# The recurrent stage's order of work: the next pair's chunk products and three of its masks ahead of the scan over states, the query products in other PSUM space

## The chip, the cores and the metric

One core of a Trainium2 chip runs the whole program. The metric is device time in microseconds. The kernel before has a median of 4070.77 us over 3 runs (4065.65 to 4073.46).

## The reference, cut to what matters

The reference is two transformer blocks of width 2048 over 256 latent tokens with 256 context tokens. The first block's token mixer has an RWKV-7 branch, which is computed in both directions for 16 heads of 64 channels. For each token the state `S` of a head is decayed, corrected and added to, and then read out:

```python
def step(S, inp):
    r_t, w_t, k_t, v_t, kk_t, a_t = inp
    sa = jnp.einsum('bhvk,bhk->bhv', S, -kk_t)
    S = (S * w_t[:, :, None, :] + sa[..., None] * (kk_t * a_t)[:, :, None, :]
         + v_t[..., None] * k_t[:, :, None, :])
    y = jnp.einsum('bhvk,bhk->bhv', S, r_t) if emit else None
```

Both blocks also need modulation vectors, `silu(c) @ w_ada + b_ada`, whose weight matrices are large (2048 x 12288 and 2048 x 6144 in float32) and are multiplied with two condition vectors only. The other parts (attention, feed-forward, the second block) are not touched by the change.

## The kernel before, in words

The program is one block with a hand-written instruction list per engine. The stage that the change touches is the recurrent one, some 650 us long (about 740 to 1390 us of the span). Its loop has eight passes, `for it in range(8)`; each handles a pair of heads (128 partitions, 64 per head) over 512 tokens (context and latents) and is called a pair here. The two directions are `d` = 0 and 1.

The tokens are cut into 8 chunks of 64 (`CH`), so that the recurrence becomes, per direction:

- `from_keys(d)` (L1107, L1112) and `chunk_pairs(d)` (L1069): products of scaled keys within a chunk; the latter fill PSUM banks `2d` and `2d+1`, 64 matmuls of 64 columns. `chunk_pairs(0)` for the next pair is issued in this pair's pass, `chunk_pairs(1)` in its own.
- Five masks on VectorE, `inverse_step(then, d, i)` with i = 0 to 4 (L2541 `aT`, L2543 `xinv`, L2545 `aT`, L2547 `xinv`, L2549 `yinv`), start the inversion of a triangular matrix. The first two read the PSUM banks of `chunk_pairs`, the others read SBUF alone.
- `level_b` (L1123), `level_xy` (L1173, L1177): five doubling levels of the inversion, each with a mask `bm` on VectorE (L2601) and copies on ScalarE.
- `solve(d)` (L1188, labels WU0, WU1): the inverse applied, into banks `2d` and `2d+1`; ScalarE (L1870) and VectorE (L2612, labels W0, W1) copy the halves to `wu`.
- `chunk_steps(d)` (L1195, L1197, L1199, labels GH0, GH1): each chunk's transition and its contribution, 96 matmuls into banks 5 and 6; VectorE turns them into `g1t` (L2617) and `hd` (L2618).
- `chunk_outputs(d)` (label Q): for the latents' chunks, query products (L1206) and the part of the output that needs no state (L1209, L1211, accumulated in the first columns of banks 2 and 3). In the kernel before, L1206 goes to banks 0 and 1; VectorE reads it in `chunk_queries` as `qt` (L2624).
- The scan over states: for i = 1 to 6 and both directions a pair of small matmuls (L1321, labels Z01 to Z16) and one VectorE instruction (`zs`, L2633). Each Z waits for the `zs` of the step before.
- `YZ` (L1334): the states' part of the output, added in banks 2 and 3. VectorE's `scaled_r` (L2518, L2519, label rs) scales the next pair's receptance; TensorE begins the next pair with `from_keys(0)` when all of VectorE's labels of this pair are done.

`scaled(d)` (L2510, L2512, L2513, L2514, label abk) makes the next pair's scaled keys `a_s`, `b_s`, `k_s` ahead of its products; `a_s` needs ScalarE's decays (label E). `bonus_keys` (L2504 to L2506) and `bv` (L2664, after the matmul L1290, label bon) are small side products.

**The modulation weights** are streamed through this stage as filling for TensorE. `ada(j, *khs)` on TensorE calls `ada_half(it, j, kh)`: per pair 3 groups (j) of 8 (kh), each one transfer of 512 KB and 8 matmuls (L826) into the first 256 columns of bank 4. Item (j, kh) is written "(2,4)" below. GpSimd issues the transfers (L679), in this order, into a ring of three buffers (`ADA_RAW = 3`). It issues item c = 8j + kh when TensorE has used item c - 3:

```python
pool.wait_ge(ada_used, 24 * it + c - ADA_RAW + 1 + 8 * ADA_HEAD)
```

After a group, `ada_take` on ScalarE (L1576) copies bank 4 out, `ada_final` on TensorE (L841, 8 small matmuls) waits for that copy and spreads the result over partitions, and `ada_bias` on VectorE (L2224, `ada(j)` there) adds the bias and lets the next group begin.

**What sets the order.** Each engine runs its list in order. The lists `RW_PE`, `RW_ACT`, `RW_DVE` hold the labels of one pass; each labelled instruction increments its engine's semaphore (`rw_pe`, `rw_act`, `rw_dve`), and `pe_at`, `act_at`, `dve_at` wait for a label's count. On VectorE each instruction of this stage waits for the one before it. On TensorE `done(mm, label)` stands behind a group of matmuls.

## Time and profile before

| | us |
|---|---|
| median of 3 runs | 4070.77 |
| lowest, highest | 4065.65, 4073.46 |
| the profiled execution | 4070.89 |
| its span on the core | 4069.2 |
| mean granted TensorE clock, share of full | 0.974 |
| TensorE matmul busy | 3844.8 |
| VectorE busy | 2497.9 |
| ScalarE busy | 1731.1 |

The profile is of one execution. PE is TensorE's matmuls, PEld its weight loads, DVE VectorE, ACT ScalarE, POOL GpSimd. A timeline row gives the start, the duration and the instruction, then in brackets how long the engine was idle before it and what ended that. "issue" means that the engine waited for nothing that the profile shows. The chain of waits is followed back from the last instruction. The clock is the share of full speed granted to TensorE. Some 1.7 us of the profiled execution lie around the span.

### The profile page before, as it was taken

The numbers are of one execution on the slowest core, as the hardware profiler recorded it, in microseconds if no ns is written. First come the engines' busy times: TensorE is split into PE (matmuls) and PEld (weight loads), VectorE is DVE, ScalarE is ACT, GpSimd is POOL, SyncE is SP. The second block draws the span as 40 slices with busy tenths as digits, with TensorE's granted clock in tenths as the row PEclk, the third lists the DMA queues.
The fourth block names the chain that finished last, engine by engine and source line by source line (L and its number), as shares of the span: only waits on it lengthen the run. The fifth ranks groups of instructions, "written<-read, shape, count | busy, mean of one in ns | idle before, by whom it ended". The sixth has DMA issues, their size and how long they took to land.

```text
span 4069.2 us, 86831 instructions
## 1 busy us (share of the span) xinstructions
PE 3844.8 (94%) x36296; PEld 3265.2 (80%) x36296; DVE 2497.9 (61%) x4413; ACT 1731.1 (43%) x3152; POOL 273.0 (7%) x437
## 2 busy tenths in 40 slices
PE   6999999789988999999999999999999999899999
PEld 3788888566666799989999999977778678787879
DVE  2544587555565677687788787764452553646365
ACT  2544333334433445446444444452342442534354
POOL 0000011222222100000000000000000000000000
PEclk8999999889999999999999999999999999999999
DMA  9422566455555587565666666532223232433335
GB/s 366 146 78 66 196 226 208 130 163 174 176 178 168 187 275 232 195 223 169 219 221 214 221 210 218 184 130 87 69 68 93 63 124 94 130 117 95 116 97 187
DMA packets 289442, 662.45 MB, mean 163 GB/s; under 512 B 21088, under 2 KB 31328, under 8 KB 287536
## 3 DMA queue, kind: packets, MB, share of 16 engines
q1 hardware_dynamic: 233392, 441.74, 33.7%
q0 software_dynamic: 55680, 215.34, 16.8%
q8 instruction: 286, 4.69, 0.5%
q14 instruction: 84, 0.69, 0.1%
HBM read 639.17 MB, written 17.83 MB: 161 GB/s over the span
## 4 chain that ended last, share of the span: by engine, by line
PE 81%; DVE 9%; ACT 4%; issue 3%; DMA 2%; SPq 0%; POOL 0%; DVEq 0%; ACTq 0%; POOLq 0%
PE psum L861 63%; PE psum L826 2%; PE psum L1123 2%; DVE wlo L2207 1%; PE psum L886 1%; PE psum L1173 1%; ACT whi L1572 1%; PE psum L841 1%; DMA ada_head<-in_w_ada 1%; PE psum L1473 1%; DVE smx L2964 1%; PE psum L1188 1%; PE psum L964 1%; PE psum L948 1%; PE psum L949 1%
## 5 line engine op out<-in xcount | busy, mean ns | idle before, releaser
L2207 DVE TENSOR_TENSOR wlo<-raw,whi 128x512 fp32r<-128x512 f32 (+3 forms) x1568 | 1049.4, 681 | 995.4 <-ACT whi L1572 985.2
L1572 ACT ACTIVATE whi<-raw 128x512 fp32r<-128x512 f32 (+3 forms) x1568 | 969.7, 623 | 1470.6 <-PE psum L861 1445.1
L861 PE MATMUL psum<-hhi,whi 128*128 128x512 f32 (+1 forms) x2416 | 831.6, 344 | 37.9 <-DVE hlo L2247 17.4
L861 PE MATMUL psum<-hhi,wlo 128*128 128x512 f32 (+1 forms) x2416 | 812.3, 336 | 0.0
L861 PE MATMUL psum<-hlo,whi 128*128 128x512 f32 (+1 forms) x2416 | 812.0, 336 | 0.0
L861 PEld LDWEIGHTS psum<-hhi,whi 128*128 128x128 f32 x2416 | 461.9, 191 | 133.5 <-issue 55.2
L861 PEld LDWEIGHTS psum<-hhi,wlo 128*128 128x128 f32 x2416 | 461.7, 191 | 47.3
L861 PEld LDWEIGHTS psum<-hlo,whi 128*128 128x128 f32 x2416 | 462.4, 191 | 46.3 <-issue 2.2
L861 PE MATMUL psum<-fhi,whi 128*128 128x256 f32 x1408 | 400.5, 284 | 19.8 <-DVE wlo L2207 15.3
L861 PE MATMUL psum<-flo,whi 128*128 128x256 f32 x1408 | 399.4, 284 | 0.0
L861 PE MATMUL psum<-fhi,wlo 128*128 128x256 f32 x1408 | 399.3, 284 | 0.0
L861 PEld LDWEIGHTS psum<-fhi,whi 128*128 128x128 f32 x1408 | 271.0, 192 | 22.2 <-DVE wlo L2207 17.3
L861 PEld LDWEIGHTS psum<-flo,whi 128*128 128x128 f32 x1408 | 271.0, 192 | 0.0
L861 PEld LDWEIGHTS psum<-fhi,wlo 128*128 128x128 f32 x1408 | 271.0, 192 | 0.0
L861 PE MATMUL psum<-uhi,whi 128*128 128x256 f32 x704 | 201.4, 286 | 5.2 <-DVE ulo L2790 5.2
L861 PE MATMUL psum<-ulo,whi 128*128 128x256 f32 x704 | 200.1, 284 | 0.0
L861 PE MATMUL psum<-uhi,wlo 128*128 128x256 f32 x704 | 200.1, 284 | 0.0
L861 PE MATMUL psum<-mixhi,whi 128*128 128x512 f32 (+1 forms) x512 | 174.3, 341 | 5.6 <-ACT stmp L2167 3.9
L861 PE MATMUL psum<-mixhi,wlo 128*128 128x512 f32 (+1 forms) x512 | 172.8, 338 | 0.0
L861 PE MATMUL psum<-mixlo,whi 128*128 128x512 f32 (+1 forms) x512 | 172.7, 337 | 0.0
L679 POOL DMA_DIRECT2D ada_raw<-in_w_ada x192 | 136.6, 711 | 404.8 <-PE psum L826 381.5
L670 POOL DMA_DIRECT2D red_raw<-in_w_adaT x128 | 67.8, 530 | 1176.1 <-DVE mod L2218 1173.9
(433 smaller groups left out, 7043.3 us busy)
## 6 DMA issues: line engine op xcount, KB each, us to landing
raw<-in_w_in SPq DMA_DIRECT2D x328, 512.0 KB, 3.9
ada_raw<-in_w_ada POOLq DMA_DIRECT2D x192, 512.0 KB, 4.5
red_raw<-in_w_adaT POOLq DMA_DIRECT2D x128, 512.0 KB, 4.7
raw<-in_w_out SPq DMA_DIRECT2D x96, 512.0 KB, 3.7
raw<-in_w_gate SPq DMA_DIRECT2D x88, 512.0 KB, 4.6
raw<-in_w_val SPq DMA_DIRECT2D x88, 512.0 KB, 4.3
raw<-in_w_down SPq DMA_DIRECT2D x88, 512.0 KB, 4.4
ada_head<-in_w_ada SPq DMA_DIRECT2D x64, 512.0 KB, 10.1
```

The source lines that it names most:

```text
L670: pool.dma_start(red_raw[m % 2][:, :], A["w_adaT"][m // 2 * P:m // 2 * P + P, m % 2 * HALF:m % 2 * HALF + HALF]).then_inc(red_in[m % 2], 16)
L679: pool.dma_start(ada_raw[c % ADA_RAW][:, :, :], A[w][256 * kh:256 * kh + 256, bass.ds(col, N)].rearrange("(a p) n -> p a n", p=P)).then_in ...
L826: mm = pe.matmul(PS[4][t:t + 32, 0:256], sc[:, 2 * kh + kk, :], src[:, kk, nh * 256:nh * 256 + 256], start=(kh == 0), stop=(kh == 7), tile ...
L841: mm = pe.matmul(PS[4][:, 256 + 2 * m:258 + 2 * m], ada_sb[:, (m % 2) * P:(m % 2) * P + P], C("sel", 4 * cond + 2 * (m // 2), 4 * cond + 2 ...
L861: mm = pe.matmul(dst, l, r, start=(k == 0 and i == 0 and first), stop=(k == nch - 1 and i == 2), skip_group_check=True)
L886: pe.matmul(PS[bank][:, 0:src.shape[-1]], ones, src, start=(j == 0), stop=(j == of - 1)).then_inc(n_mm, 1)
L948: pe.matmul(PS[4 + u % 2][:, :], qn[a % 2][:, h, q0:q0 + P], k_sb[a % 2][:, h, :], start=True, stop=False)
L949: pe.matmul(PS[4 + u % 2][:, :], qpad[a % 2][:, h, q0:q0 + P], kpe[:, :], start=False, stop=True).then_inc(mla_pe, 1)
L964: mm = pe.matmul(PS[7][:, 0:TOK], v_sb[a % 2][:, kt, h * P:h * P + P], (probT, probT2)[h][:, kt, :], start=(kt == 0), stop=(kt == 3))
L1123: return pe.matmul(PS[2 * d][HS[1 - e if l == 1 else e], ch(g)], aT[d][HS[1 - e], g, :], xinv[d][HS[1 - e], g, :], start=True, stop=True)
L1572: act.activation(whi[:, lc % HL, 0:width], raw[:, (lc // 2) % RAW, lc % 2, 0:width], ACT.Copy).then_inc(w_hi, 1)
L2207: dve.tensor_tensor(wlo[:, lc % HL, 0:width], raw[:, (lc // 2) % RAW, lc % 2, 0:width], whi[:, lc % HL, 0:width].bitcast(F32), ALU.subtrac ...
```

## The change

On TensorE, `chunk_pairs(done, 0)` for the next pair moves from behind the scan's first step to ahead of `chunk_steps(0)`. The items of the third modulation group change places: (2,0) to (2,7) were spread from ahead of the gate product to the scan's third step; now (2,0) stands between the two solves, (2,1) and (2,2) behind `chunk_steps(1)`, and (2,3) to (2,7) one behind each of the scan's steps 1 to 5. The second group's `ada_final` moves behind `bon` and `level_xy(1, 5)`, the third group's behind `YZ`. The query products L1206 go to banks 2 and 3, columns 256 and up. On VectorE the first three of the next pair's five masks move ahead of the scan, the other two stand behind its steps 2 and 3; the first two instructions of `scaled(1)` move ahead of W1, and `bonus_keys` ahead of the bias `ada(1)`. The number of instructions stays the same. Below, the signs at the left mark removed and added lines:

```diff
@@ -454,6 +454,10 @@
         def scan_steps(*more):
             return [f"Z{d}{i}" for i in range(1, 7) for d in range(2)] + list(more)

+        def scan_with(label, step):
+            z = scan_steps()
+            return z[:2 * step] + [label] + z[2 * step:]
+
         FIRST_PE = ["kn", "w0", "w1", "a0", "a1", "kx", "al0"]
         FIRST_ACT = ["sq", "kn", "nx", "w0", "w1", "a0", "a1", "E0", "E1", "dc"]
         FIRST_DVE = ["rc", "L0", "L1", "kd", "kk", "bt", "abk0", "abk1", "rs", "I0"]
@@ -462,12 +466,12 @@
         RW_PE += ["B03", "kn", "B13", "ta1", "X03", "Y03", "w0", "X13", "Y13", "tb1"]
         RW_PE += ["B04", "P10", "w1", "B14", "a0", "X04", "Y04", "tk1", "X14", "Y14", "a1"]
         RW_PE += ["B05", "P11", "kx", "Y05", "B15", "bon", "Y15", "g"]
-        RW_PE += ["WU0", "WU1", "GH0", "Q", "GH1", "Z01", "Z11", "al0"] + scan_steps("YZ")[2:]
+        RW_PE += ["WU0", "WU1", "al0", "GH0", "Q", "GH1"] + scan_steps("YZ")
         RW_ACT = ["v", "ta0", "X01", "Y01", "tb0", "X11", "Y11", "sq", "X02", "Y02", "tk0", "X12", "Y12", "sd", "kn"]
         RW_ACT += ["ta1", "X03", "Y03", "w0", "X13", "Y13", "tb1", "P10", "w1", "a0", "nx", "X04", "Y04", "tk1", "X14", "Y14", "a1", "E0"]
         RW_ACT += ["P11", "Y05", "Y15", "gs", "E1", "WU0", "WU1", "yc", "dc"]
         RW_DVE = ["I1", "B01", "B11", "ar0", "B02", "B12", "ce", "ar1", "B03", "B13", "rc", "out", "L0", "B04", "B14", "L1", "kd"]
-        RW_DVE += ["B05", "kk", "B15", "bv", "bt", "abk0", "W0", "W1", "abk1", "GH0", "Q", "GH1"] + scan_steps("I0", "rs")
+        RW_DVE += ["B05", "kk", "B15", "bv", "bt", "abk0", "W0", "W1", "abk1", "GH0", "Q", "GH1"] + scan_with("I0", 3) + ["rs"]
         LAST_PE, LAST_ACT, LAST_DVE = ["mn", "vr"], ["sd"], ["ce", "out"]
         RW_END = len(FIRST_DVE) + 8 * len(RW_DVE) + len(LAST_DVE)

@@ -1203,10 +1207,10 @@

                     for b in range(2):
                         for h, e in TILES4:
-                            mm = pe.matmul(PS[e][HS[h], ch(2 * d + b)], wu[d][HS[e], h, 2 + b, 0:64], arx[d][HS[e], h, b, :], start=True, stop=True)
+                            mm = pe.matmul(PS[2 + e][HS[h], ch(4 + 2 * d + b)], wu[d][HS[e], h, 2 + b, 0:64], arx[d][HS[e], h, b, :], start=(d == 0 and b == 0), stop=True, skip_group_check=True)
                     for b in range(2):
                         for h, e in TILES4:
-                            pe.matmul(PS[2 + e][HS[h], ch(b)], v_tok[HS[e], 2 + b, HS[h]], arx[d][HS[e], h, 2 + b, :], start=(d == 0 and b == 0), stop=False, skip_group_check=True)
+                            pe.matmul(PS[2 + e][HS[h], ch(b)], v_tok[HS[e], 2 + b, HS[h]], arx[d][HS[e], h, 2 + b, :], start=False, stop=False, skip_group_check=True)
                         for h, e in TILES4:
                             mm = pe.matmul(PS[2 + e][HS[h], ch(b)], wu[d][HS[e], h, 2 + b, 64:P], arx[d][HS[e], h, b, :], start=False, stop=False, skip_group_check=True)
                     return mm
@@ -1285,11 +1289,10 @@
                 ada(1, 6)
                 last_y_b()
                 ada(1, 7)
-                ada_final(it * 3 + ADA_HEAD + 1, 0)
                 act_at("a1")
                 done(pe.matmul(PS[6][:, 0:TOK], bones, bonus[:, :], start=True, stop=True), "bon")
                 level_xy(1, 5)
-                ada(2, 0)
+                ada_final(it * 3 + ADA_HEAD + 1, 0)
                 dve_at("kk")
                 pe.wait_ge(rw_in2, it * 32 + 32)
                 if it == 0:
@@ -1299,33 +1302,27 @@
                 done(mm, "g")

                 solve(0)
-                ada(2, 1)
+                ada(2, 0)
                 solve(1)
-                ada(2, 2)
                 dve_at("W0")
                 act_at("WU0")
+                chunk_pairs(done, 0)
                 chunk_steps(0)
-                ada(2, 3)
                 dve_at("W1")
                 act_at("WU1")
                 chunk_outputs(0)
                 done(chunk_outputs(1), "Q")
-                ada(2, 4)
                 dve_at("GH0")
                 chunk_steps(1)
-                ada(2, 5)
+                ada(2, 1, 2)
                 for i in range(1, 7):
                     for d in range(2):
                         dve_at(f"GH{d}" if i == 1 else f"Z{d}{i - 1}")
                         for h in range(2):
                             mm = pe.matmul(PS[(7, 5)[d]][HS[h], ch(i % 2)], g1t[d][HS[h], SCAN[d][i], :], state(d, i)[HS[h], :], start=True, stop=True)
                         done(mm, f"Z{d}{i}")
-                    if i == 1:
-                        chunk_pairs(done, 0)
-                    if i in (1, 3):
-                        ada(2, 5 + (i + 1) // 2)
-                    if i == 6:
-                        ada_final(it * 3 + ADA_HEAD + 2, 1)
+                    if i < 6:
+                        ada(2, 2 + i)
                 dve_at("Z16")
                 for i in range(4, 8):
                     for d in range(2):
@@ -1333,6 +1330,7 @@
                         for h in range(2):
                             mm = pe.matmul(PS[2 + c % 2][HS[h], ch(c // 2)], state(d, i)[HS[h], :], qt[d][HS[h], ch(c)], start=False, stop=(i == 7 and d == 1), skip_group_check=True)
                 done(mm, "YZ")
+                ada_final(it * 3 + ADA_HEAD + 2, 1)

             RW_ACT_END, RW_DVE_END = 8 * len(RW_ACT) + len(FIRST_ACT), 8 * len(RW_DVE) + len(FIRST_DVE)

@@ -2621,7 +2619,7 @@

                     pe_at("Q")
                     for d in range(2):
-                        t = TT(bec(qt[d]), eb(0, d * P, P), bec(r_s[d]), ALU.add)
+                        t = TT(bec(qt[d]), eb(2, 256 + d * P, P), bec(r_s[d]), ALU.add)
                         if d == 0:
                             own.then(t)
                     done(t, "Q")
@@ -2662,22 +2660,30 @@
                 level(1, 5)
                 pe_at("bon")
                 done(TT(bv[:, :], PS[6][:, 0:TOK], v_t[:, TOK:T2], ALU.mult), "bv")
+                bonus_keys(done)
                 ada(1)
-                bonus_keys(done)
                 scaled(done, 0, act_at)
                 solved(0)
+                own.then(TT(b_s[1][:, :], kk[:, :], icl[1][:, :], ALU.mult))
+                act_at("E1")
+                own.then(STT(a_s[1][:, :], kk[:, :], -1.0, l_ex[1][:, :], ALU.mult, ALU.mult))
                 solved(1)
-                scaled(done, 1, act_at)
+                own.then(TT(b_s[1][:, :], b_s[1][:, :], l_in[1][:, :], ALU.mult))
+                done(TT(k_s[1][:, :], kdir[1][:, :], l_in[1][:, :], ALU.mult), "abk1")
+                pe_at("al0")
+                inverse_step(own.then, 0, 0)
+                inverse_step(own.then, 0, 1)
                 chunk_steps(0)
+                inverse_step(own.then, 0, 2)
                 chunk_queries()
                 chunk_steps(1)
                 for i in range(1, 7):
                     for d in range(2):
                         state(d, i)
-                    if i == 1:
-                        pe_at("al0")
-                    else:
-                        inverse_step(own.then if i < 6 else lambda ins: done(ins, "I0"), 0, i - 2)
+                    if i == 2:
+                        inverse_step(own.then, 0, 3)
+                    if i == 3:
+                        inverse_step(lambda ins: done(ins, "I0"), 0, 4)
                 scaled_r(done)
                 ada(2)
             last_done = lambda ins, label: (ins.then_inc(rw_dve, 1), dve.wait_ge(rw_dve, at(LAST_DVE, label, 0, 8 * len(RW_DVE) + len(FIRST_DVE))))
```

## Rows read from the trace of the kernel before

**Rows 1.** The page of the whole execution: the span, TensorE's busy time.

```profile
span 4069.2 us, 86831 instructions
...
PE 3844.8 (94%) x36296; PEld 3265.2 (80%) x36296; DVE 2497.9 (61%) x4413; ACT 1731.1 (43%) x3152; POOL 273.0 (7%) x437
```

**Rows 2.** Stretches: length us; busy (x) of PE, PEld, DVE, ACT, POOL; clock, DMA, GB/s.

```profile
790.30:873.60 83.30, 72.73 (x1920) 52.87 (x1917) 46.23 (x83) 29.24 (x53) 21.89 (x32) 0.92 0.56 167
...
1114.80:1192.70 77.90, 70.76 (x1928) 51.24 (x1926) 46.20 (x83) 29.24 (x53) 21.85 (x32) 0.96 0.59 175
...
1272.20:1352.50 80.30, 72.49 (x1926) 52.05 (x1927) 46.04 (x82) 29.35 (x53) 21.83 (x32) 0.91 0.58 172
```

**Rows 3.** Waits of TensorE in the stage, 740 to 1390 us: total, times, longest.

```profile
PE psum L1069 <- issue: 4.9, 3, 2.2
PE psum L841 <- ACT ada_sb L1576: 4.0, 8, 0.5
PE psum L1195 <- issue: 3.6, 2, 2.9
...
PE psum L826 <- DMA ada_raw<-in_w_ada: 1.8, 5, 0.6
```

**Rows 4.** Timeline of TensorE, third pair: start us, us, instruction, [idle before].

```profile
951.48 0.64 PE L826 MATMUL psum<-ada_raw,sc 128*32 128x256 f32 x8
952.62 1.05 PE L841 MATMUL psum<-con,ada_sb 128*128 128x2 f32 x8 [0.50 <-ACT ada_sb L1576]
...
959.32 1.96 PE L1188 MATMUL psum<-atok_r,yinv 64*64 64x128 f32 x32
961.21 0.64 PE L826 MATMUL psum<-ada_raw,sc 128*32 128x256 f32 x8
```

**Rows 5.** Timeline of VectorE in the same pair.

```profile
954.32 0.42 DVE L2664 TENSOR_TENSOR bv<-psum,v_t 128x256 f32<-128x256 f32 x1 [1.93 <-PE psum L1290]
...
956.20 0.69 DVE L2510 TENSOR_TENSOR b_s<-kk,icl 128x512 f32<-128x512 f32 x1
...
961.40 0.69 DVE L2612 TENSOR_SCALAR wu<-psum 128x512 f32<-128x512 f32 x1 [1.60 <-PE psum L1188]
...
969.34 0.69 DVE L2617 TENSOR_TENSOR g1t<-psum,con 128x512 f32<-128x512 f32 x1 [1.97 <-PE psum L1199]
...
974.47 0.60 DVE L2633 SCALAR_TENSOR_TENSOR zs<-psum,dec,hd 128x64 f32<-128x64 f32 x2 [2.91 <-PE psum L1321]
975.11 0.69 DVE L2541 TENSOR_TENSOR aT<-psum,con 128x512 f32<-128x512 f32 x1
...
981.30 0.42 DVE L2518 TENSOR_TENSOR r_s<-r_t,sig 128x256 f32<-128x256 f32 x1
```

**Rows 6.** The chain of waits in the same pair: start us, us, what.

```profile
967.53 0.79 issue
...
971.14 0.93 PE psum L1069 x61
...
985.23 1.14 PE psum L1069 x64
```

**Rows 7.** Timeline of TensorE from the second direction's chunk steps to the next pair.

```profile
969.16 0.64 PE L826 MATMUL psum<-ada_raw,sc 128*32 128x256 f32 x8
...
979.49 1.36 PE L841 MATMUL psum<-con,ada_sb 128*128 128x2 f32 x8
980.78 1.86 PE L1334 MATMUL psum<-qt,zs 64*64 64x64 f32 x29
982.34 0.36 PE L1107 MATMUL psum<-a_s,k_s 64*64 64x64 f32 x1
```

**Rows 8.** Timeline of GpSimd, same pair: an issue for `ada_raw`.

```profile
962.62 0.70 POOL L679 DMA_DIRECT2D ada_raw<-in_w_ada  x1 [1.75 <-PE psum L826]
```

**Rows 9.** The tile `ada_raw` in the stage, from issue to landing.

```profile
DMA to landing us min/median/max: 3.9/4.5/7.0
```

**Rows 10.** The third pair's scan as one stretch, columns as in rows 2.

```profile
969.10:983.00 13.90, 10.40 (x205) 7.29 (x202) 9.28 (x22) 0.58 (x2) 2.18 (x4) 0.89 0.47 145
```

## The prediction, made before the changed kernel had run

> **What bounds the kernel now.** I began with the page. The span is 4069.2 us, in a profiled execution of 4070.9 that stands at the median of the runs (4070.8), and TensorE is busy for 94% of it [rows 1]. Then I cut the recurrent stage into stretches from one pair's `bv` to the next. They last 77.9 to 83.3 us, 80.3 in the mean of the seven, and TensorE's sum is only 71 to 73 of that [rows 2]; so 7 to 11 us of a pair is time in which TensorE has nothing to do. Last, the waits: 4.9 us before L1069 and 3.6 us before L1195 are gaps without a releaser (instruction supply), ScalarE's copy holds the final product of a modulation group 0.5 us in each pair, and loads of `ada_raw` hold TensorE hardly at all, 1.8 us in the whole stage [rows 3]. The reader is to see that the streamed weights are just in time today. The rest is seen in one pair, the third, in time order. All times below are of that pair; E is the end of item (1,7), which starts at 951.48 and hands on at 952.1 [rows 4].
>
> **Ahead of the scan.** *The second group's final product* moves behind `bon` and `level_xy`. It waited 0.50 us for ScalarE and started at 952.62 [rows 4]. Now `bon` starts at E. L1290 is the release of `bv` at 954.32 [rows 5]; without the wait and the some 0.9 us of L841, `bv` starts at 952.9. The final product follows `level_xy`, finds its copy made, and costs its own time only. *Item (2,1)* leaves the place between the solves' end and the chunk steps, and (2,0) stands where (2,1) was; an item hands on after 0.57 us of its 0.64. TensorE's list between E and the end of the second solve thus loses 0.50 of waiting and one item: 1.07 us. The second solve, which started at 959.32 and took 1.96 [rows 4], ends near 960.2, and W1, which waited for it until 961.40 [rows 5], can start at 960.3.
>
> *VectorE.* From `bv` to the first `b_s` is 1.88 us (954.32 to 956.20) [rows 5], and that stays, as the bias only changes places with `bonus`: `b_s` at 954.8. Operations of 512 columns follow each other every 0.725 us (0.69 busy). Four for `scaled(0)`, then W0, then the two that were moved ahead of W1: 954.8 + 7 x 0.725 = 959.9, so W1 still waits, until 960.3. Behind it stand now W1, two operations of `scaled(1)`, two masks, `g1t` and `hd`: seven, as before (W1, four, `g1t`, `hd`). The wait is over 1.1 us earlier, and so is all behind it: `hd` of direction 0 ends at 965.4, not 966.5. Two of the moved masks thus cost nothing, since they stand in for the two operations pulled into W1's wait. The third and `qt` (0.73 + 0.91) end at 967.0, under TensorE's second `chunk_steps`.
>
> *TensorE beneath that.* From 960.2 it has the moved products of 64 matmuls (1.14 us [rows 6]), the first chunk steps (about 1.6) and the outputs (1.5): it is through at 964.5, some 0.9 us ahead of `hd`. That cover hides the move of the products; a supply gap over 0.9 us would show. In this pair the second chunk steps had such a gap of 0.79 us [rows 6]. Without it they take 1.77 us, and item (2,1) starts behind them at 967.0. I call this time a. The item at that place, (2,5) before, started at 969.16 [rows 7], or 968.4 without the gap. **The front half thus gains 1.35 us a pair.** Moving L1206 to banks 2 and 3 costs nothing by itself: the same 32 matmuls, and VectorE's reads have the same size. It is what lets the products into banks 0 and 1.
>
> **The scan.** Before, step 1's `zs` was followed by the products (0.93 of them in the chain [rows 6]), an item and a supply gap, so that VectorE sat idle 2.91 us before step 2 [rows 5]. Then each step was two `zs` (0.60) and a mask (0.69), 1.36 us, and `r_s` began at 981.30 [rows 5]. With products and three masks gone, steps of 1.0 to 1.36 us would end the scan about a + 8.2. That is where the change is meant to gain, and where I see **the next thing that is late: the ring of three buffers**.
>
> Seven items now stand from a to the scan's end. Three are loaded at a, (2,1), (2,2) and (2,3). Item (2,4) needs the buffer of (2,1). GpSimd issues when an item has been used: the item of 961.21, over at 961.85, is followed by the issue at 962.62 [rows 4, 8], 0.77 later. Landing comes 3.9 to 7.0 us after the issue, 4.5 in the median [rows 9]; for a queue that has just run empty I take 4.2, near the lower end. So (2,4) starts at a + 0.64 + 0.77 + 4.2 = a + 5.6, where the scan would want it near a + 3.5. (2,5) and (2,6) were issued behind it and land some 2 us apart, near a + 7.5 and a + 9.3; the steps between run under these waits. (2,7) needs the buffer of (2,4): a + 5.6 + 0.64 + 0.77 + 4.2 = a + 11.2. It stands ahead of Z06 and Z16 on TensorE, hence ahead of the last `zs`, YZ, ScalarE's copy `yc` and `rs`. It is used by a + 11.85, the last step takes 0.9, and YZ starts at a + 12.9 and issues for 1.6 (980.78 to 982.34 [rows 7]). The final product, which lay in the shade of the last `zs` and now does not, adds 0.8 (1.36 at the low clock [rows 7]). The next pair starts at **a + 15.4**. Bounds: a + 14.7 with landings of 3.9, a + 17 with 5.0. Before, it started at 982.34, that is 13.2 behind 969.16, and 13.7 in the mean of the pairs, as most have more supply gaps there. **The back half loses 1.7 us a pair.**
>
> No landing under 3.9 us was seen in the stage [rows 9], so I give one sooner no chance of its own beyond rival 1 below. The page "DMA: Bandwidth & Descriptors" of the Trainium skill, section "Anatomy of one DMA — SWDGE (gpsimd) path", fits a transfer as 2.0 us plus its size over 436 GB/s, by estimate 3.2 us for 512 KB. By that figure the two rounds would be 2 us shorter and the sum would come out near -1 us a pair, 4062 us, as in rival 1. The trace does not agree: its landings, counted from GpSimd's issue, are all longer.
>
> **Clock.** In the scan the granted clock was 0.89 in the mean [rows 10], so part of it ran at 1.2 GHz, and an item or a final product is then longer (L841 1.36 us against some 0.8). With TensorE waiting longer I expect more of the scan there: nothing to 1.0 us a pair, two items and the final product at 0.4 to 0.5 each; I take 0.5.
>
> **Sum.** -1.35 + 1.7 + 0.5 = +0.85 us a pair, times 8 = +7 us, and nothing behind the stage changes. 4070.9 + 7 = **4078 us**. Its own range is 4072 to 4090. A measurement of this kernel can tell about 0.2% from no change, 8 us; my forecast lies at that line.
>
> **Rivals.** (1) *The waits swallow the supply gaps; faster.* The gaps before L1069, L1195 and others are 1 to 2 us a pair [rows 3]. If they fall under the load waits, or vanish as the queues are empty at a, and landings take 3.9, then a pair gives -1.35 + 1.0 - 0.8 = -1.15: 4062 us. It decides when the gaps ahead of a are below the 0.9 us of cover. Against it: the products are now among the dense small matmuls ahead of a, where a gap moves the whole chain of two rounds. 20%. (2) *No load wait*: if the items came in time, the scan would end at a + 8.2 and the next pair start at a + 11, so -1.35 - 2.7 = -4: 4038 us. For it, only that 1.8 us of load waits were seen [rows 3]; against it, the two rounds follow from the code and the shortest landing. 8%. (3) *Slow landings, supply gaps ahead of a and low clock together*, from landings over 4.8 us when three are in flight: back half +2.8, clock +1.0, gaps +0.4, so +2.9 a pair: 4094 us. For it: landings up to 7.0 [rows 9]. 22%. (4) The forecast, 50%, half of it within 0.2% and half above.
>
> **Numbers.** Faster by over 0.2%: rival 2 and most of rival 1, 0.20. Within 0.2%: the rest of rival 1 and over half of the forecast, 0.33. Slower: the rest, 0.47. The range reaches from rival 1 with a margin to just above rival 3: 4056 to 4098.
>
> **What would show it.** Right: TensorE waits for `ada_raw` twice or more in each pair's scan, some 5 to 8 us a pair in place of 1.8 us in the stage; `bv` 1.4 us earlier behind (1,7); `g1t` of direction 1 above 2 us earlier in this pair; no wait of L841 for ScalarE; GpSimd's issues bunched behind a. Wrong: no load waits before L826 (then rival 2), W1 still the end of a wait of 1.6 us, or supply gaps of over 2 us a pair ahead of a.

## The result, and the profile after it

The changed kernel takes 4101.18 us in the median of 4 runs (4092.55 to 4104.99), against 4071.5 before (4 runs). The ratio is 1.0072, with an interval of 1.0056 to 1.0088: **0.7% slower**. The profiled execution took 4102.6 us with a span of 4100.9, 31.7 more than before. I had forecast 4078 with a range of 4056 to 4098: the sign that held the largest chance was right, the size was not, and the range missed it by 3 us.

The changed kernel has other line numbers. L830 is a modulation item, L845 a final product, L1199 to L1203 the chunk steps, L1210 the query products, L1213 and L1215 the part of the output that needs no state, L1322 the scan, L1331 YZ and L1111 the next pair's first product. A gap of TensorE that the profile puts down to no releaser ("issue") is called a supply gap below; the name is my reading, and no run shows what these gaps are.

TensorE's waits in the stage of the changed kernel, 735 to 1430 us (total, times, longest), answer to [rows 3]:

```profile
PE psum L830 <- DMA ada_raw<-in_w_ada: 34.1, 23, 4.0
PE psum L1127 <- DVE yinv L2547: 13.0, 8, 1.6
PE psum L1210 <- issue: 7.1, 3, 2.7
...
PE psum L1213 <- issue: 3.9, 2, 2.0
PE psum L1203 <- issue: 3.7, 3, 1.7
PE psum L1201 <- issue: 2.6, 2, 2.4
```

Two things are to be seen. Load waits grew from 1.8 to 34.1 us. And the supply gaps, which were spread over the scan and what lay ahead of it, now lie on the chunk steps, query products and outputs ahead of the scan (L1201 to L1213). No wait of L845 for ScalarE is left.

VectorE in the third pair, answering to [rows 5] (E, the end of item (1,7), is 959.65 here and 952.12 before):

```profile
960.39 0.43 DVE L2662 TENSOR_TENSOR bv<-psum,v_t 128x256 f32<-128x256 f32 x1 [0.54 <-PE psum L1293]
...
962.45 0.17 DVE L2222 TENSOR_TENSOR mod<-psum,vec 128x8 f32<-128x8 f32 x1 [0.33 <-PE psum L845]
962.54 0.68 DVE L2508 TENSOR_TENSOR b_s<-kk,icl 128x512 f32<-128x512 f32 x1
...
967.79 0.69 DVE L2610 TENSOR_SCALAR wu<-psum 128x512 f32<-128x512 f32 x1 [0.21 <-PE psum L1192]
...
972.84 0.69 DVE L2615 TENSOR_TENSOR g1t<-psum,con 128x512 f32<-128x512 f32 x1 [1.45 <-PE psum L1203]
...
977.61 0.69 DVE L2615 TENSOR_TENSOR g1t<-psum,con 128x512 f32<-128x512 f32 x1 [1.71 <-PE psum L1203]
...
983.99 0.60 DVE L2631 SCALAR_TENSOR_TENSOR zs<-psum,dec,hd 128x64 f32<-128x64 f32 x2 [2.29 <-PE psum L1322]
```

TensorE in the same scan, answering to [rows 7]:

```profile
977.44 1.07 PE L830 MATMUL psum<-ada_raw,sc 128*32 128x256 f32 x16
...
982.97 0.64 PE L830 MATMUL psum<-ada_raw,sc 128*32 128x256 f32 x8 [2.61 <-DMA ada_raw<-in_w_ada]
983.54 0.45 PE L1322 MATMUL psum<-zs,g1t 64*64 64x64 f32 x8
985.45 1.08 PE L830 MATMUL psum<-ada_raw,sc 128*32 128x256 f32 x8 [1.47 <-DMA ada_raw<-in_w_ada]
...
987.09 1.08 PE L830 MATMUL psum<-ada_raw,sc 128*32 128x256 f32 x8
...
988.76 1.08 PE L830 MATMUL psum<-ada_raw,sc 128*32 128x256 f32 x8
...
991.03 1.97 PE L1331 MATMUL psum<-qt,zs 64*64 64x64 f32 x32 [0.56 <-DVE zs L2631]
992.93 1.86 PE L845 MATMUL psum<-con,ada_sb 128*128 128x2 f32 x8
```

The four rows of L830 from 982.97 are (2,4) to (2,7). The first waits 2.61 us for its load, the second 1.47, and from there an item takes 1.08 us, not 0.64: the granted clock was at 1.2 GHz from 984.0 to 997.7. In this pair (2,7) did not wait. YZ and the final product stand bare between the last `zs` and the next pair. GpSimd's issues say why the loads come late (they stand for (2,3), for (2,4) and (2,5) together, for (2,6) and for (2,7)):

```profile
966.54 0.71 POOL L683 DMA_DIRECT2D ada_raw<-in_w_ada  x1 [4.30 <-PE psum L830]
978.83 1.45 POOL L683 DMA_DIRECT2D ada_raw<-in_w_ada  x2 [11.58 <-PE psum L830]
980.74 0.72 POOL L683 DMA_DIRECT2D ada_raw<-in_w_ada  x1 [0.46 <-issue]
984.37 0.70 POOL L683 DMA_DIRECT2D ada_raw<-in_w_ada  x1 [2.91 <-PE psum L830]
```

For 12 us nothing is issued, because no item is used; then three loads are asked for in 2 us, and the fourth only once (2,4) has been used. In the whole stage, from issue to landing:

```profile
DMA to landing us min/median/max: 3.8/4.3/6.8
```

The clock of the stage, as stretches of the kernel before and after (columns as in [rows 2]); the granted clock has two levels here, full and half, so by estimate 0.93 means that 14% of the time ran at 1.2 GHz, and 0.89 means 22%:

```profile
740.00:1390.00 650.00, 582.41 (x15372) 423.82 (x15366) 374.39 (x663) 238.63 (x431) 171.01 (x251) 0.93 0.57 169
```

```profile
740.00:1420.00 680.00, 591.17 (x15327) 425.13 (x15323) 371.95 (x661) 235.26 (x427) 171.16 (x250) 0.89 0.53 160
```

The means over the eight pairs, worked out from the timelines as times behind E (the next pair's first product and the length are means of seven, since the last pair has no next; gaps and waits are TensorE's gaps of over 0.1 us between E and that first product). Rows of seven and of eight pairs can't be subtracted from each other, so the way from the last `zs` to the next product has a row of its own:

| us behind E | before | after |
|---|---|---|
| `bv` | 2.25 | 0.78 |
| W1 | 9.31 | 8.22 |
| second `g1t` | 17.30 | 16.88 |
| end of the last `zs` | 28.55 | 30.99 |
| YZ starts | 29.31 | 31.05 |
| next pair's first product | 31.21 | 34.79 |
| last `zs` to the next product, pair by pair | 2.36 | 3.75 |
| length of a pair | 80.37 | 84.27 |
| supply gaps ahead of the second `g1t` / in all | 0.96 / 1.70 | 2.43 / 2.47 |
| load waits | 0.00 | 4.11 |

So a pair is 3.9 us longer. Over the seven pairs that have a next one: -0.6 up to the second `g1t`, +2.8 in the scan (11.4 to 14.2), +1.4 from the last `zs` to the next product, +0.3 in the rest. (Over all eight pairs the second `g1t` gained 0.42 and the scan lost 2.86.) Eight times 3.9 is the 31 us.

### The profile page after: what moved, and what is told of

Same layout as the page of the kernel before. It is cut to its first block, busy times and chain, and to the rows that moved or that the text cites. A ratio compares the mean times of both kernels' runs of the same rounds, so it can differ in the third digit from the quotient of the medians.

```text
span 4100.9 us, 86839 instructions
## 1 busy us (share of the span) xinstructions
PE 3858.9 (94%) x36296; PEld 3271.1 (80%) x36296; DVE 2497.9 (61%) x4413; ACT 1730.7 (42%) x3152; POOL 273.4 (7%) x437
## 4 chain that ended last, share of the span: by engine, by line
PE 82%; DVE 8%; ACT 4%; DMA 3%; issue 3%; SPq 0%; POOL 0%; POOLq 0%; DVEq 0%; ACTq 0%
PE psum L865 62%; PE psum L830 3%; DMA ada_raw<-in_w_ada 2%; PE psum L1127 2%; DVE wlo L2205 1%; PE psum L890 1%; PE psum L1177 1%; PE psum L845 1%; ACT whi L1570 1%; DMA ada_head<-in_w_ada 1%; PE psum L1471 1%; DVE smx L2970 1%; PE psum L968 1%; PE psum L952 1%; PE psum L953 1%
## 5 line engine op out<-in xcount | busy, mean ns | idle before, releaser
L865 PEld LDWEIGHTS psum<-fhi,whi 128*128 128x128 f32 x1408 | 271.9, 193 | 22.2 <-DVE wlo L2205 17.3
L830 PE MATMUL psum<-ada_raw,sc 128*32 128x256 f32 x1536 | 140.4, 444 | 35.0 <-DMA ada_raw<-in_w_ada 34.1
```

Of the source, the lines that this page charges most:

```text
L830: mm = pe.matmul(PS[4][t:t + 32, 0:256], sc[:, 2 * kh + kk, :], src[:, kk, nh * 256:nh * 256 + 256], start=(kh == 0), stop=(kh == 7), tile ...
L865: mm = pe.matmul(dst, l, r, start=(k == 0 and i == 0 and first), stop=(k == nch - 1 and i == 2), skip_group_check=True)
```

## The experiments

All ran beside the kernel before on the same chips; ratios are to it. Its median was 4075.65, 4073.16 and 4075.03 us in the three rounds, against 4071.5 beside the changed kernel, so a difference in us between runs of different rounds, and a miss of an interval by 1 to 3 us, is not told from nothing. The table gives the median, the ratio with its interval, and the same per-pair means, which are those of the profiled execution. Its time stands in brackets: in four runs it lies 7 to 11 us from the median (moves_old_bias and half_load_ring3 above, thin_front and old_products_new_items below). "`zs` to product" is taken pair by pair, from the end of the last `zs` to the next pair's first product.

| run | us (profiled) | ratio | second `g1t` | last `zs` ends | `zs` to product | gaps ahead | load waits |
|---|---|---|---|---|---|---|---|
| moves_only | 4080.9 (4079.9) | 1.0013 (1.0004 to 1.0022) | 21.68 | 29.97 | 2.74 | 2.44 | 0.10 |
| moves_old_bias | 4071.3 (4078.9) | 0.9998 (0.9989 to 1.0007) | 21.04 | 29.21 | 2.53 | 2.65 | 0.14 |
| items_only | 4091.3 (4091.9) | 1.0038 (1.0023 to 1.0052) | 16.29 | 30.64 | 3.20 | 1.26 | 4.11 |
| half_ring6 | 4016.5 (4014.5) | 0.9858 (0.9844 to 0.9872) | 16.09 | 24.35 | 2.12 | 2.06 | 0.00 |
| half_load_ring3 | 4041.9 (4052.4) | 0.9921 (0.9906 to 0.9935) | 16.01 | 27.91 | 2.82 | 1.85 | 2.36 |
| final_ahead | 4086.4 (4088.2) | 1.0030 (1.0019 to 1.0041) | 16.77 | 30.83 | 2.54 | 2.61 | 4.53 |
| thin_front | 4096.1 (4085.7) | 1.0054 (1.0038 to 1.0069) | 15.72 | 29.75 | 3.29 | 1.00 | 4.37 |
| spread | 4071.5 (4071.4) | 0.9987 (0.9975 to 0.9999) | 17.40 | 26.96 | 4.57 | 2.15 | 1.06 |
| tail_items2 | 4062.9 (4064.2) | 0.9974 (0.9964 to 0.9984) | 17.61 | 26.56 | 2.90 | 2.02 | 0.43 |
| products_under | 4069.4 (4068.4) | 0.9988 (0.9979 to 0.9997) | 16.07 | 27.10 | 2.79 | 1.42 | 0.27 |
| products_under_late | 4061.2 (4064.4) | 0.9966 (0.9955 to 0.9977) | 15.87 | 26.25 | 3.77 | 1.67 | 0.04 |
| old_products_new_items | 4077.4 (4066.1) | 1.0007 (0.9996 to 1.0018) | 16.75 | 27.58 | 2.97 | 1.56 | 0.10 |

**moves_only** keeps the moves and puts the items back.

```diff
                 chunk_pairs(done, 0)
                 chunk_steps(0)
+                ada(2, 3)
...
-                ada(2, 1, 2)
+                ada(2, 5)
...
-                    if i < 6:
-                        ada(2, 2 + i)
+                    if i in (1, 3):
+                        ada(2, 5 + (i + 1) // 2)
+                    if i == 6:
+                        ada_final(it * 3 + ADA_HEAD + 2, 1)
```

> The changed kernel, with all items of the modulation weights and both final products at the places that they had in the kernel before; the products, the masks and the other PSUM space stay changed. Ring theory (the lateness comes from seven items asking a ring of three buffers within one scan): load waits on TensorE fall from 34 us in the stage to under 4 us, the scan from the second direction's g1t to the end of the last zs takes 8 to 9 us in place of 14, and the time is 4040 to 4055 us, faster than both. Supply theory (the lateness comes from dense small matmuls brought together ahead of the scan): the supply gaps ahead of the scan stay at 2 to 2.5 us a pair and the time is 4085 to 4100 us.

The load waits went, 0.10 us a pair, and the scan took 8.3 us: there the ring theory held. Its time did not: 4080.9, not under 4055. The second `g1t` came at 21.7 us in place of 17.3. One part was my edit: (2,0) waits for the bias of the second group (7.0 us in eight waits), which the change had put behind `bonus`. The next run undoes that.

**moves_old_bias** is moves_only with these lines:

```diff
-                bonus_keys(done)
                 ada(1)
+                bonus_keys(done)
```

> The run moves_only with the second group's bias again ahead of bonus on VectorE; in moves_only item (2,0) waited for that bias, and W1 came 1.2 us later than in the kernel before. Theory of a full front (with the products and three items ahead of hd, TensorE itself ends the front, and its supply gaps are no longer covered): W1 is back at 9.3 us behind E, but the second direction's g1t stays at 19 to 21 us behind E against 17.3 before, and the scan is 3 us shorter: 4065 to 4076 us. If the bias was all that held moves_only: 4040 to 4055 us.

4071.3 us, level with the kernel before, as the theory of a full front said. The second `g1t` stays at 21.0, and the scan takes 8.2 us in place of 11.25. (W1 was not quite back: 9.3 in four of eight pairs, but 9.96 in the mean; in the two latest pairs, with 12.4 and 10.7, the granted clock was low for 3.4 us or more ahead of it.) TensorE has 1.14 us of products more ahead of `hd`, so I take it that it ends the front itself and pays each supply gap there in full. **What the moves save in the scan they cost ahead of it, unless items leave the front.** That is the link between the two halves of the change.

**items_only** is the kernel before with the changed places of items, final products and bias:

```diff
-                ada(2, 5)
+                ada(2, 1, 2)
...
-                    if i in (1, 3):
-                        ada(2, 5 + (i + 1) // 2)
-                    if i == 6:
-                        ada_final(it * 3 + ADA_HEAD + 2, 1)
+                    if i < 6:
+                        ada(2, 2 + i)
...
                 done(mm, "YZ")
+                ada_final(it * 3 + ADA_HEAD + 2, 1)
```

> The kernel before, with only the items, both final products and the bias placed as in the changed kernel; products, masks and query products stay where they were. Ring theory: nearly the whole loss is here, 4092 to 4105 us, with some 30 us of load waits, since products and masks in the scan fall under those waits. Supply theory: the products are back behind the scan's first step, so the gaps ahead of the scan fall back to 1 us a pair, and the time is 4065 to 4080 us.

TensorE waits just as long for loads with the products in their old place. The time, 4091.3, lies 1 us under the ring theory's interval and 11 over the supply theory's. The supply gaps ahead of the scan are 1.26 us, 1.2 less a pair than in the changed kernel, which would be some 9 of the 10 us between the two. So both theories hold a part, the ring the larger.

**half_ring6** shortens the loads and deepens the ring in the same 12 KB of each partition:

```diff
-ADA_RAW = 3
+ADA_RAW = 6
...
-                pool.dma_start(ada_raw[c % ADA_RAW][:, :, :], A[w][256 * kh:256 * kh + 256, bass.ds(col, N)].rearrange("(a p) n -> p a n", p=P)).then_inc(ada_in[c % ADA_RAW], 16)
+                pool.dma_start(ada_raw[c % ADA_RAW][:, :], A[w][256 * kh:256 * kh + 128, bass.ds(col, N)]).then_inc(ada_in[c % ADA_RAW], 16)
```

> The changed kernel, but each item loads only the first half of its weights (256 KB) and TensorE multiplies that half twice, so the modulation vectors leave out half of the sum; the 12 KB of the three buffers are cut into a ring of six. TensorE's instructions are the same in number and order. Ring theory: items are loaded well ahead, the load waits vanish (under 2 us in the stage) and a pair loses the 4.1 us of waits and some low clock: 4055 to 4070 us. Supply theory: the gaps ahead of the scan stay and only the waits' part goes, but the time stays over 4085 us. Clock theory (the low clock comes from elsewhere than the load waits): the last item to the next pair's first product stays at 3.7 us from YZ's start.

**half_load_ring3** has the half loads and three buffers.

> The changed kernel with half of each item's load (256 KB, TensorE multiplies that half twice, so half of the modulation sum is left out), and the ring kept at three buffers. It parts the depth of the ring from the size of a transfer. Depth theory (two rounds of hand-back, issue and landing follow each other within the scan, however small the load): (2,4) and (2,7) still end load waits, 1.5 to 3 us of load waits a pair, and 4045 to 4070 us, at least 25 us behind the run with six buffers (4016.5). Size theory (bytes in flight make the landings late): load waits under 0.5 us a pair and within 10 us of that run.

With six buffers the waits are gone and the time is 4016.5, 84.7 us under the changed kernel and 39 under my interval. With three it is 4041.9 and 18.8 us of load waits stay in the stage. The landing took 2.7, 3.0 and 5.1 us (min, median, max) for 256 KB with three buffers, 2.8, 3.2 and 5.1 with six, and 3.8, 4.3 and 6.8 for 512 KB; GpSimd's issue took 0.54 us for 256 KB and 0.72 for 512. So the depth alone is 25 us, as the depth theory asked, though the time lies 3 us under its interval, and the size alone, with three buffers, is 59; both count. What I had not priced is the clock. TensorE around YZ of half_ring6:

```profile
953.09 0.64 PE L830 MATMUL psum<-ada_raw,sc 128*32 128x256 f32 x8
...
954.76 1.15 PE L1331 MATMUL psum<-qt,zs 64*64 64x64 f32 x32 [0.66 <-DVE zs L2631]
955.84 1.05 PE L845 MATMUL psum<-con,ada_sb 128*128 128x2 f32 x8
```

```profile
740.00:1325.00 585.00, 531.77 (x15203) 384.88 (x15204) 366.64 (x653) 233.10 (x423) 133.79 (x243) 1.00 0.33 99
```

YZ takes 1.15 us in place of 1.97, the final product 1.05 in place of 1.86. The granted clock was 1.00 over the stage, so practically all of it ran at 2.4 GHz, while in the kernel before and in every other run it fell in every pair or nearly. From YZ to the next pair's product it is 2.1 us, 1.6 less than in the changed kernel, with the same instructions in the same order. The clock theory's 3.7 did not stay. Nor does the gain lie between E and the next product alone: of the 10.9 us by which a pair is shorter than in the changed kernel, 2.6 lie behind that product, where the changed kernel still ran at 1.2 GHz for 4.0 us and this one never did.

At the same load size, the ring of three still has load waits, 2.4 us a pair, and the clock of its profiled execution is that of the kernel before (it was the slowest of four; over the whole kernel its clock was 0.976, that of the others 0.978 to 0.98, that of half_ring6 0.983 to 0.984):

```profile
740.00:1364.00 624.00, 558.75 (x15204) 399.55 (x15200) 367.64 (x654) 232.74 (x420) 136.37 (x247) 0.93 0.32 94
```

So with half loads the low clock went with the waits, and halved bytes alone did not take it away. Load waits are not all of it: with full loads and hardly any load wait, moves_old_bias (0.14) and products_under_late (0.04) have 0.93 and 0.94, and there TensorE waits 1.7 and 1.3 us a pair in the scan for VectorE, against 0.5 in half_ring6. Six buffers with full loads were not run, so what the halved bytes have in it is not shown.

**final_ahead** puts the third final product back:

```diff
                     if i < 6:
                         ada(2, 2 + i)
+                    else:
+                        ada_final(it * 3 + ADA_HEAD + 2, 1)
...
                 done(mm, "YZ")
-                ada_final(it * 3 + ADA_HEAD + 2, 1)
```

> The changed kernel with the third group's final product back ahead of YZ, as in the kernel before. From the end of the last zs to the next pair's first product it was 3.80 us in the changed kernel and 2.66 before. If it is the place of the final product that costs (it lost its cover under the last zs), this comes back to 2.7 to 3.2 us, 5 to 8 us in all: 4093 to 4096. If it is the low clock alone, nothing changes: 4099 to 4102.

4086.4 us: 15 less than the changed kernel, twice what its place was to give, and 7 under that interval. From the last `zs` to the next product it is 2.5 us, 1.2 less a pair than in the changed kernel and near the 2.4 of before; that is some 10 us. (The 3.80 and 2.66 in the expectation are differences of means over seven and eight pairs; pair by pair they are 3.75 and 2.36.) Most of the rest lies behind the next product, 0.4 us a pair, where the low clock lasts 2.9 us in place of 4.0. The stage's clock is 0.92 in place of 0.89:

```profile
740.00:1402.00 662.00, 570.73 (x15305) 411.57 (x15299) 369.45 (x656) 234.22 (x425) 171.39 (x251) 0.92 0.54 164
```

**thin_front** leaves out 64 matmuls a pair from the front:

```diff
-                    for b in range(2):
-                        for h, e in TILES4:
-                            pe.matmul(PS[2 + e][HS[h], ch(b)], v_tok[HS[e], 2 + b, HS[h]], arx[d][HS[e], h, 2 + b, :], start=False, stop=False, skip_group_check=True)
-                        for h, e in TILES4:
-                            mm = pe.matmul(PS[2 + e][HS[h], ch(b)], wu[d][HS[e], h, 2 + b, 64:P], arx[d][HS[e], h, b, :], start=False, stop=False, skip_group_check=True)
```

> The changed kernel with the 64 matmuls a pair (L1213, L1215) left out that add the part of the output that needs no state; the output lacks that part. TensorE was not the end of the front by its own work (0.9 us of cover), so without supply gaps this takes nothing off. Supply theory: gaps ahead of the scan (2.4 us a pair) fall by 1 us or more and the second g1t comes at 15.2 to 16 us behind E in place of 16.9, 4086 to 4094 us. If the gaps cost nothing: 4098 to 4103 us.

The gaps ahead fell to 1.00 us and the second `g1t` came at 15.7, as the supply theory said. TensorE now waits for `hd` ahead of the second chunk steps, 11.7 us in six waits, so it has its cover back. The median, 4096.1, lies between the two intervals, but these means are those of the profiled execution, the fastest of the four with 4085.7, at the lower edge of the supply theory's interval; the other three took 4094.7 to 4099.6. So the gaps' price in `g1t` is shown, and their price in time stays open.

**spread** hands the items out again; the products stay ahead.

```diff
                 chunk_pairs(done, 0)
+                ada(2, 1)
                 chunk_steps(0)
+                ada(2, 2)
...
-                ada(2, 1, 2)
+                ada(2, 3)
...
-                    if i < 6:
-                        ada(2, 2 + i)
+                    if i in SPREAD:
+                        ada(2, SPREAD[i])
```

with `SPREAD = {1: 4, 2: 5, 4: 6, 6: 7}`.

> The changed kernel with the third group's items spread again: (2,0) between the solves, (2,1) behind the products, (2,2) behind the first chunk steps, (2,3) behind the second, (2,4), (2,5), (2,6), (2,7) behind the scan's steps 1, 2, 4 and 6; the final products as in the changed kernel. Ring theory: no item is asked for under 5.6 us after its buffer was handed back by much, so load waits stay under 8 us in the stage, the front half keeps its 1.1 us gain per pair, and the time is 4040 to 4060 us. Supply theory: within 8 us of the changed kernel's 4101 us.

30 us off the changed kernel by places of items alone; but 4071.5, not under 4060. Load waits were 9.9 us in the stage, not under 8, and the front's gain did not stay: the second `g1t` came at 17.4. (2,7) behind step 6 held YZ by 1 us, and YZ and the final product still ran bare at the low clock, 3.6 us a pair.

**tail_items2** takes both out of there:

```diff
                 done(mm, "YZ")
+                ada(2, 7)
...
                 from_keys(0)
-                ada(0, 0)
+                if it:
+                    ada_final(it * 3 + ADA_HEAD - 1, 1)
                 pe.wait_ge(v_in, it * 16 + 16)
                 turn(v_t, "trv")
+                ada(0, 0)
```

with `SPREAD = {1: 4, 2: 5, 4: 6}`.

> As the run spread, but item (2,7) stands behind YZ and the third group's final product behind the next pair's from_keys(0), with (0,0) behind the transposes of v; (2,6) behind step 4 stays. Theory (ring depth, and what stands uncovered between the last zs and the next pair): the 4.9 us from the last zs to the next pair's first product in spread fall to about 2, of which an item and a final product (1.4 us) come back behind it as plain work; 2 us a pair less than spread: 4050 to 4062 us. If supply gaps rule, within 6 us of spread (4071).

From the last `zs` to the next product (with (2,7) in it) it is 2.9 us in place of 4.6, not the 2 expected, and 4062.9 us, 1 over the interval: **faster than the kernel before**, ratio 0.9974 (0.9964 to 0.9984).

**products_under** and **products_under_late** move the products behind the second chunk steps, and the masks back into the scan:

```diff
-                chunk_pairs(done, 0)
                 chunk_steps(0)
...
                 chunk_steps(1)
-                ada(2, 1, 2)
+                chunk_pairs(done, 0)
...
-                    if i == 2:
-                        inverse_step(own.then, 0, 3)
-                    if i == 3:
-                        inverse_step(lambda ins: done(ins, "I0"), 0, 4)
+                    if i == 1:
+                        pe_at("al0")
+                    if i < 6:
+                        inverse_step(own.then if i < 5 else lambda ins: done(ins, "I0"), 0, i - 1)
```

> As tail_items2, but the next pair's chunk products stand behind the second direction's chunk steps, where TensorE waits 1.4 us for g1t and hd, and all five masks are in the scan again (one behind each of steps 1 to 5); items (2,1) behind the first chunk steps, (2,2) behind the query products, (2,3) behind the moved products, (2,4), (2,5), (2,6) behind steps 1, 3, 5, (2,7) behind YZ. Theory of a full front (TensorE, not VectorE, ends the front once products and items are ahead of hd): the second g1t comes 1 us a pair earlier than in tail_items2, the scan's steps stay near 1.36 us, and the time is 4048 to 4060 us. If masks in the scan are what matters, the scan from the last zs of step 1 on gets over 1 us longer than the 6.6 us there and the time is 4065 to 4075.

> As products_under with one item fewer ahead of hd: (2,1) behind the query products, (2,2) behind the moved products, (2,3), (2,4), (2,5) behind steps 1, 3 and 5, (2,6) and (2,7) behind YZ. Theory of a full front: another 0.5 us a pair off the front, given back behind YZ as plain work: within 5 us of products_under. Ring theory: at this spacing no load waits over 1 us a pair.

The second `g1t` came 1.5 us earlier than in tail_items2, but the end of the last `zs` did not (27.1 against 26.6). Supply gaps now fell behind the products (1.1 us a pair up to step 1's `zs`, in place of 0.4), and that `zs` came 3.4 us behind `g1t` in place of 2.4. From there to the end of the scan it took 7.6 us in place of 6.6, where the masks are back. So 4069.4, a miss of the front theory's interval; both signs of the other one, masks in the scan, came in (over 1 us more than 6.6, and 4065 to 4075). With one item less ahead it is 4061.2, 8 us lower where I had expected at most 5, ratio 0.9966 (0.9955 to 0.9977), the lowest of all full kernels. Its interval overlaps that of tail_items2, so the two are not told apart; products_under is slower than both in the median.

**old_products_new_items** is the control for where that gain comes from: tail_items2's finals and tail with the products and masks of the kernel before.

```diff
-                    if i in (1, 3):
-                        ada(2, 5 + (i + 1) // 2)
-                    if i == 6:
-                        ada_final(it * 3 + ADA_HEAD + 2, 1)
+                    if i in (1, 3):
+                        ada(2, 4 + (i + 1) // 2)
...
                 done(mm, "YZ")
+                ada(2, 7)
```

> The kernel before with its products and masks in their old places, but the second final product behind level_xy, the items of the third group one place earlier or later so that they stay spread, (2,7) behind YZ and the third final product behind the next from_keys(0). If the gain of tail_items2 over the kernel before comes from the items and final products alone, this gives 4055 to 4065 us too; if it needs the moved products and masks, 4068 to 4078.

4077.4 us, inside the second interval, ratio 1.0007 (0.9996 to 1.0018). These places of the items alone bring nothing, as the moves alone brought nothing (moves_old_bias). Only both together do, 0.3% at the most.

## Why the prediction was right or wrong

- **The front up to the first `g1t`, where no gap fell, was right to 0.1 us.** `bv` at 0.8 behind E (0.74 in seven of eight pairs), W1 at 8.2 (8.14 in six), the first `g1t` at 11.8 (in six of eight; in the third pair gaps made it 13.2). From `bv` to `b_s` it took 2.15 us in the third pair, not 1.88, since the bias waited 0.33 us for the moved final product, but W1's wait took that up. Two masks cost nothing, and the query products' new place cost nothing that the runs show.
- **"The front half thus gains 1.35 us a pair": wrong, 0.4.** By my own rows it was 1.1: the second chunk steps took 2.66 us from 966.50 to 969.16, 1.87 without the gap, so item (2,1) would start at 967.3, not 967.0. The step that failed beyond that is the 0.9 us of cover over supply gaps. I had put the gaps ahead of the scan at about their old size; they grew from 0.96 to 2.43 us a pair. They went with the place of the products: with them ahead of the scan the gaps there were 1.9 to 2.7 us a pair in every run but thin_front, also where items stood between (moves_old_bias 2.65, spread 2.15). With the products behind the second chunk steps or later they were 1.0 to 1.7, and with 64 other matmuls left out 1.0. In all, the gaps grew by 0.8 us a pair; the other half of the 1.47 is that they moved to where nothing hides them. thin_front (gaps 1.00, `g1t` 1.2 earlier) and items_only (1.26, 0.6 earlier) bear that out. I had the mechanism in rival 3 at 0.4 us.
- **The ring of three: right mechanism, the rounds too short.** (2,4) ended a load wait in all eight pairs, (2,5) in seven and (2,7) in five, not in the third. Without waits (half_ring6) the scan from `g1t` takes 8.3 us, near what I had put for that case (8.2 from a). The landings that I took at 4.2 were 4.09 and 4.34 in the third pair. (2,4) was to start 5.6 us behind a and started 6.0, (2,7) 11.2 and 12.1, YZ 12.9 and 14.3. I read the 1.4 us as what follows a landing at the low clock, items of 1.08 us in place of 0.64, and as the second load, (2,5), which landed 5.8 us after its issue; no run parts the two.
- **The final product behind YZ and the clock: mis-sized.** I had 1.6 us for YZ and 0.8 for the final product, and 0.5 for the clock over all. Measured from YZ to the next product: 3.7, and 2.1 at the full clock in half_ring6. My 0.8 was a price at the full clock in a place where the clock was low; the row of 1.36 stood beside it in my own text. final_ahead prices that one line at 15 us.
- **The sum.** Over the seven pairs: front -0.6 for -1.35; from a to the next product 18.15 us for 15.4 + 0.5; the rest of the pair +0.3, for which I had nothing. Before, that way took 13.97 us in the mean, not the 13.7 that I took, so the back half lost 4.2 where I had 1.7 + 0.5. My third rival, slow landings with gaps ahead and the low clock, had -1.35 + 0.4 + 2.8 + 1.0 = 2.9 a pair, and 3.9 came. It came nearest, but only in part for its reason: of its landings of over 4.8 us only that of (2,5) held TensorE in the third pair, and the median was 4.3. The 20% for load waits that swallow the gaps was wrong in kind: gaps came ahead of the waits, not under them.
- The fit of the page "DMA: Bandwidth & Descriptors" of the Trainium skill, section "Anatomy of one DMA — SWDGE (gpsimd) path", by estimate 3.2 us for 512 KB and 2.6 for 256 KB, is under the medians here, 4.3 and 3.0 counted from GpSimd's issue, and under the minima of 3.8 and 2.7.

Still open: what the supply gaps are, what part of final_ahead's 15 us is the clock itself, and whether six buffers of full loads would bring what half_ring6 brought.

## What to carry to other kernels

Work used as filling has a supply of its own: count how many pieces fall into one stretch, how many buffers are loaded ahead, and add hand-back, issue and landing for each round beyond; bunching the same pieces cost 30 us here, and spreading them (spread) gave it back. Before work is moved from behind a wait to ahead of it, ask whether the engine has room there with its usual gaps, and move something out for it: the moves alone gave nothing, the spread items alone gave nothing, and both together 0.3%. What stands behind the last result of a chain is paid at the clock that is granted there, so read that stretch's clock before it is priced.

## What the runs showed of the hardware that I had not expected

In half_ring6 the granted clock over the stage was 1.00, while it fell in every pair of the kernel before, though TensorE waited for loads only 1.8 us in the whole stage there; it has short waits for VectorE in the scan, 12.1 us in 24 waits for `zs`, none over 0.7. That the clock went by them is not shown. The 32 matmuls of YZ took 1.15 us in half_ring6 and 1.97 in the changed kernel, and the eight of a final product 1.05 and 1.86. Between E and the next pair's first product TensorE stood still without a releaser for 1.0 to 2.8 us of a pair in the mean, whatever the order, among its 64x64 matmuls above all (the least with 64 of them left out); halving the loaded bytes took little of that away (2.3 us a pair in half_ring6 and 2.0 in half_load_ring3, against 2.5 in the changed kernel).
